# Strides kept as (group, d) on the partitions, 64-row compression products, and the sample convolution moved behind attention

## The reference

```python
s = k_raw[:, :n_str * CMP_STRIDE].reshape(B, n_str, CMP_STRIDE, G, Dh)   # stride, token in stride, group, d
w1r = w1.reshape(CMP_RATIO, CMP_STRIDE, Dh, Dh)                          # 2 halves x 16 x 64 x 64
pre = jnp.einsum('bnlgd,lde->bnge', s[:, 0:nb], w1r[0]) + b1
for r in range(1, CMP_RATIO):
    pre = pre + jnp.einsum('bnlgd,lde->bnge', s[:, r:r + nb], w1r[r])
return jnp.einsum('bnge,ef->bngf', jax.nn.silu(pre), w2)
```

## Time and profile before

| | us |
|---|---|
| median of 3 runs | 831.82 (830.76 to 832.16) |
| the profiled execution, its own time | 829.77 |
| span of its instructions | 828.0 |
| PE busy | 774.4 (94% of the span) |
| DVE busy | 375.8 (45%) |
| ACT busy | 220.5 (27%) |
| POOL busy | 166.9 (20%) |

### The profile page before, as it was taken

One profiled execution on the slowest core, in us unless ns is written; L12 is line 12 of the kernel. 1 busy time (PEld: TensorE's weight loads), 2 busy tenths in 40 slices (PEclk: granted clock), 3 DMA queues, 4 the chain that ended last, 5 costly groups with the idle time before them and its releaser, 6 DMA issues.

```text
span 828.0 us, 11541 instructions
## 1 busy us (share of the span) xinstructions
PE 774.4 (94%) x4479; PEld 541.6 (65%) x4479; DVE 375.8 (45%) x799; ACT 220.5 (27%) x480; POOL 166.9 (20%) x270
## 2 busy tenths in 40 slices
PE   5999999997999999999999999999999899998763
PEld 3657778876766667777767777774456855555431
DVE  2201899999778880111006552231227632222106
ACT  3000324252256662233125640000001112221113
POOL 2338447100200006000005420002000213222010
PEclk9999999998999999999999999999999999999889
DMA  9676445130270005152214529703105999999847
GB/s 314 166 15 189 140 102 159 45 112 1 68 277 2 2 2 180 51 179 76 77 51 132 177 89 297 288 1 115 51 26 208 385 386 413 406 405 395 322 149 263
DMA packets 87505, 138.98 MB, mean 168 GB/s; under 512 B 25493, under 2 KB 60465, under 8 KB 86287
## 3 DMA queue, kind: packets, MB, share of 16 engines
q1 hardware_dynamic: 71439, 101.41, 35.7%
q0 software_dynamic: 11392, 32.71, 13.3%
q10 hardware_dynamic: 4616, 4.08, 1.6%
HBM read 132.00 MB, written 21.14 MB: 185 GB/s over the span
## 4 chain that ended last, share of the span: by engine, by line
PE 79%; DMA 8%; DVE 7%; issue 4%; SPq 1%; ACT 1%; ACTq 0%; POOL 0%; DVEq 0%; POOLq 0%
PE ps L1914 17%; PE ps L2099 15%; PE ps L2357 7%; PE ps L2435 6%; PE ps L1938 5%; PE ps L2012 4%; PE ps L2451 3%; DMA mgT<-w_up 2%; PE ps L2142 2%; PE ps L2117 2%; DVE cv L1399 2%; PE ps L2130 2%; DMA arena<-w_up 2%; DMA arena<-yscratch 2%; PE ps L2425 1%
## 5 line engine op out<-in xcount | busy, mean ns | idle before, releaser
L2099 PE MATMUL ps<-xT,keep 128*128 128x288 f32 x512 | 126.9, 408 | 0.8 <-ACT h L1210 0.5
L2099 PEld LDWEIGHTS ps<-xT,keep 128*128 128x128 f32 x512 | 96.7, 190 | 27.2 <-ACT h L1210 0.9
L1914 PE MATMUL ps<-xT,arena 128*128 128x288 f32 x384 | 95.4, 408 | 0.6 <-DVE keep L1492 0.6
L1914 PEld LDWEIGHTS ps<-xT,arena 128*128 128x128 f32 x384 | 72.3, 190 | 20.0 <-issue 0.8
L1399 DVE SCALAR_TENSOR_TENSOR cv<-keep,cv 128x512 f32<-128x512 f32 x120 | 83.7, 749 | 1.4
L2357 PE MATMUL ps<-arena,xT 128*128 128x512 f32 x128 | 55.4, 592 | 0.0
L2435 PE MATMUL ps<-keep,mgT 128*64 128x256 f32 x224 | 42.9, 396 | 2.1 <-DMA mgT<-w_up 2.1
L1938 PE MATMUL ps<-mgT,xT 128*128 128x512 f32 (+1 forms) x128 | 44.4, 507 | 0.0
L2357 PEld LDWEIGHTS ps<-arena,xT 128*128 128x128 f32 x128 | 24.2, 190 | 29.2 <-issue 29.1
L842 ACT ACTIVATE mgT<-ps 64x512 f32<-64x512 f32 x56 | 33.1, 591 | 32.3 <-PE ps L1992 31.7
L1280 ACT ACTIVATE keep<-h 128x1024 f32<-128x1024 f32 (+1 forms) x5 | 5.3, 1057 | 130.1 <-DVE h L1705 121.5
(11 more groups left out here) (409 smaller groups left out, 1337.7 us busy)
## 6 DMA issues: line engine op xcount, KB each, us to landing
arena<-w_down SPq DMA_DIRECT2D x19, 512.0 KB, 16.7
keep<-w_in SPq DMA_DIRECT2D x16, 512.0 KB, 3.9
arena<-w_gate SPq DMA_DIRECT2D x15, 512.0 KB, 8.6
arena<-w_up SPq DMA_DIRECT2D x15, 512.0 KB, 12.2
keep<-w_gate SPq DMA_DIRECT2D x14, 512.0 KB, 11.5
keep<-w_up SPq DMA_DIRECT2D x14, 512.0 KB, 17.0
h<-x_prompt SPq DMA_DIRECT2D x8, 512.0 KB, 5.2
arena<-w_in SPq DMA_DIRECT2D x8, 512.0 KB, 8.0
```

What stands on the lines that cost most here:

```text
L1914: last = mm(tokens(j)[:, b, :], weights(k), halves(x[:, k, :])[:, b, :], start=k == 0, stop=k == n_k - 1)
L2099: last = mm(out[:, 0:half], wmg[n // 2 % 3][:, k, :], xT[:, k, (n % 2) * half:(n % 2 + 1) * half], start=k == 0, stop=k == KD - 1, skip_gr ...
```

## The change

1. XT becomes partition (group, d), then token in stride, stride: what a turned job has already. `spread` and `spread_own` become one copy each.
2. The compression product takes one token of the stride at a time: 16 matmuls of 64 rows for each group and column range in place of 8 of 128 rows, the two groups alternating, group 0 in the rows 0 to 63 of the array and group 1 in 64 to 127. Both groups' jobs are claimed together and filled by the last pair.
3. The weights stand twice, once for each group's partitions, in three pieces of 8, 4 and 4 tokens in free memory: 12 transfers instead of 2 for each of w_ck1 and w_cv1, of 1 MB instead of 0.5 MB.
4. Before attention PE does the last query projection and the last two rope products ahead of the second compression product. The small products on the compressed values go behind the first two units' scores, in place of the 18 unread transposes, and their evictions stand between the exps (ACT) and after the first normalization (DVE). A table AT_ENTRY gives the slots there, and attention waits slot by slot instead of for all four.
5. The samples' convolution stands in one piece behind attention. "mean" goes from behind 4 gates to behind 8, "var" from behind 10 to behind 14, and the third kind of cached keys from behind 8 to behind 6.
6. The first two merge weights and the gathers of cached keys no longer wait for the samples' convolution; the third merge weight gets a new place and waits for the last rope job.

```diff
-        XT = cut(0, NKV, KD, STR, base=mg_flat)
+        XT = cut(0, 2 * KD, STR, base=mg_flat)
-        w1 = cut(4096, KD, P)
+        w1 = [(8, cut(4096, 8, P)), (4, cut(HPG * (T + SEQ), 4, P, base=h_flat)), (4, cut(2 * KD * STR, 4, P, base=mg_flat))]
+        w1_row = [w[:, x, :] for n, w in w1 for x in range(n)]
...
             def compress_weights(name):
-                for r in range(2):
-                    sp.dma_start(w1[:, :, r * HD:(r + 1) * HD],
-                                 a[name][0, r * 16:(r + 1) * 16].rearrange("(j q) d e -> (q d) j e", q=2)).then_inc(s_w1, 16)
+                x = 0
+                for n, w in w1:
+                    for g in range(NKV):
+                        for r in range(2):
+                            sp.dma_start(w[g * HD:(g + 1) * HD, :, r * HD:(r + 1) * HD],
+                                         a[name][0, r * 16 + x:r * 16 + x + n].rearrange("j d e -> d j e")).then_inc(s_w1, 16)
+                    x += n
...
         def spread(copy, how, j, u):
-            for q in range(2):
-                for g in range(NKV):
-                    v = slot(j)[g * HD:(g + 1) * HD, :].rearrange("p (k q s) -> p k q s", q=2, s=P)[:, :, q, :]
-                    k0 = (u % 2) * (KD // 2)
-                    last = copy(XT[q * HD:(q + 1) * HD, g, k0:k0 + KD // 2, (u // 2) * P:(u // 2 + 1) * P], v, *how)
-            return last
+            rows = slice((u % 2) * KD, (u % 2 + 1) * KD)
+            return copy(XT[:, rows, (u // 2) * P:(u // 2 + 1) * P], slot(j).rearrange("p (k s) -> p k s", s=P), *how)
...
             def compress_first(n):
...
-                for g in range(NKV):
-                    j = first_job(n, g)
+                out = [first_job(n, g) for g in range(NKV)]
+                for j in out:
                     claim(pe, j)
-                    for lo, hi in ((0, STR_S // 2), (STR_S // 2, STR)):
-                        for k in range(KD):
-                            last = mm(strides_at(j)[:, lo:hi], w1[:, k, :], XT[:, g, k, lo:hi], start=k == 0, stop=k == KD - 1)
-                    fill(last, j)
+                for lo, hi in ((0, STR_S // 2), (STR_S // 2, STR)):
+                    for x in range(16):
+                        for g in range(NKV):
+                            r = slice(g * HD, (g + 1) * HD)
+                            last = mm(strides_at(out[g])[:, lo:hi], w1_row[x][r, :], XT[r, x, lo:hi], start=x == 0, stop=x == 15)
+                            if x == 15 and hi == STR:
+                                fill(last, out[g])
...
-            for j in range(J_ATT - SLOTS, J_ATT):
-                result_of(pe, j)
+            result_of(pe, JOB["rope", 2])
             cmp_scores(0)
+            result_of(pe, JOB["w1", 1])
             scores(0)
+            result_of(pe, JOB["w1own", 1])
             scores(1)
-            for _ in range(18):
-                tr(turned[0][:, 0:P], ident[:, :], ident[:, :])
+            sample_values()
+            prompt_values()
             cmp_turns(0)
+            result_of(pe, JOB["w2", 1])
...
             keys_turned(0)
+            dve.wait_ge(s_pv, NU)
+            conv_sample(0, DS)
             j = JOB["mean"]
             result_of(dve, j)
...
-            conv_done(pool)
             pool.wait_ge(s_cso, 16 * (1 + DB))
+            result_of(pool, JOB["ga", CC - 2], JOB["ga", CC - 1])
             for b in range(2):
                 gather("cache_k_sel", kraw[b], b, s_kin[b])
```

More of the change, by code:

```diff
@@ L315, in build @@
         qtmp = cut(12416, 2, T)
-        wmg = [cut(1024 * s, KD, P, base=k2) for s in range(3)]
+        wmg = [cut(1024 * s, KD, P, base=k2) for s in range(2)] + [cut(2080, KD, P, base=k3)]
         PT = [cut(6400 + 1024 * s, NKV, 512) for s in range(2)]
@@ L648, in values_window @@
                     sp.dma_start(vwin[:, b, :, :], svw[:, n, :, :]).then_inc(s_vw, 16)
-            conv_done(sp)
+            for c in range(CC):
+                sp.wait_ge(s_tap[c], TAPS)
             take(sp, JOB["cso"])
-            for n in range(3):
+            for n in range(2):
                 mg_weights(n)
+            result_of(sp, JOB["rope", HPG - 1])
+            mg_weights(2)
+            sp.wait_ge(s_anew, CC)
             sp.wait_ge(s_kvout, 16 * N_KVOUT)
@@ L1124, in _ @@
             spread_raw(1, 5, 7)
+            queries(3)
             upper_halves(1)
             compress_silu(1)
-            queries(3)
-            j = JOB["w2", 1]
-            take(act, j)
-            give(nc.scalar.activation(vcS[:, :, :].rearrange("p b n -> p (b n)"), slot(j)[0:HD, :], ACT.Copy), j)
             def merge_gate(n, src):
@@ L1176, in _ @@
             exps(0)
+            j = JOB["w2", 1]
+            take(act, j)
+            give(nc.scalar.activation(vcS[:, :, :].rearrange("p b n -> p (b n)"), slot(j)[0:HD, :], ACT.Copy), j)
             exps(1)
@@ L1212, in _ @@
             keys_turned(0, 0)
-            merge_gates(*range(4))
+            merge_gates(*range(6))
+            keys_turned(0, 2)
+            merge_gates(6, 7)
             j = JOB["mean"]
@@ L1234, in _ @@
                 nc.scalar.activation(cv[:, c, :], cv[:, c, :], ACT.Silu, scale=cng[:, c:c + 1], bias=cnb[:, c:c + 1]).then_inc(s_silc, 1)
-            merge_gates(*range(13, 22))
+            merge_gates(*range(17, 22))
             small_exps(0)
@@ L1501, in _ @@
             rotated(2)
-            conv_sample(0, 5)
+            rotated(3)
             compress_pre(1)
-            conv_sample(5, DS)
-            j = JOB["w2own"]
-            take(dve, j)
-            for g in range(NKV):
-                r = slice(g * STR_P, (g + 1) * STR_P)
-                last = V.tensor_copy(vcB[r, g * HD:(g + 1) * HD], slot(j)[r, g * HD:(g + 1) * HD])
-            give(last, j)
-            rotated(3)
             def maxima(u):
@@ L1556, in _ @@
             normalize(0)
+            j = JOB["w2own"]
+            take(dve, j)
+            for g in range(NKV):
+                r = slice(g * STR_P, (g + 1) * STR_P)
+                last = V.tensor_copy(vcB[r, g * HD:(g + 1) * HD], own_values(j)[r, g * HD:(g + 1) * HD])
+            give(last, j)
             for u in range(NU):
```

76 lines of the change are left out of this document (39 added, 37 removed).

## The result

| kernel | median us (lowest to highest, runs) | ratio to before, 95% interval |
|---|---|---|
| before | 831.82 (829.53 to 834.29, 7) | 1 |
| changed | 824.84 (823.56 to 828.2, 7) | 0.9916, 0.9897 to 0.9936 |

Forecast were 822.7 us, in a range of 819.2 to 827.0. The kernel is 7.0 us faster (5.3 to 8.6), where 9.1 were forecast. The profiled execution took 824.84 us, its span is 823.1.

What follows compares the result with a forecast made beforehand. The chain of waits was taken to run through PE, then DVE up to the second compression product. First score 9.2 us earlier less 0.1 for the entry gives 9.1; 831.82 less 9.1 is 822.7 us, range 819.2 to 827.0.

Steps and rivals of the forecast that it cites:

- Product: Each compression product takes 14.9 us at full clock because half-height pairs overlap; bounds 14.7 to 18.2, without overlap 29.4.
- PE late next: Ahead of the second compression product PE becomes late; third queries wait 1.65 us, the product runs from 200.2 to 215.1.
- Entry: From the second product's end to the second unit's turns: 12.0 us where it was 11.9; bounds 10.5 to 14.
- larger gain: Rival: attention's entry takes 10.5 us as value products keep the clock full; 1.5 to 2 us more, 820.9; chance 0.10.
- Behind attention: The samples' convolution, 20.3 us on DVE, ends at 337.8 before PE wants it for "mean" at 348.1; costs nothing.
- The sum ahead of attention: Attention's first score 9.2 us earlier, less 0.1 for the entry: 9.1 us gained.
- a gain ahead of attention should reach the end undiminished: Later stages start from results of earlier ones, so the whole 9.1 us was counted in the total.
- cheaper evictions: On DVE up to the second product, single copies replace the strides' evictions and save 4.1 us against 1.05 lost.
- ahead of attention the same 20.3 us on DVE gave PE nothing: Moving the samples' convolution from ahead of attention gains PE nothing; its wait at 224.29 was for the last rotation only.
- No overlap: Rival in the compression products: the array's halves don't work together; 29.4 us more, 852.1; chance 0.06.
- POOL and DVE hold each other up: Rival behind attention: DVE slowed, PE waits 10 us for "mean", 832.7; chance 0.03. If POOL suffers, nothing is lost.
- The clock or the entry takes a part back: Rival in attention's entry: PE's three waits halve the clock for longer, price 2 to 4 us, 825.5; chance 0.15.

Runs made afterwards that it cites:

- serial_groups: Changed kernel with its 128 half-height products issued group after group, so neighbours never use different row halves; 851.91 us, ratio 1.0215.
- order_only: Changed kernel with its new order but the strides' old layout, copies and full-height products; 822.0 us, ratio 0.9874.
- after_c: Changed kernel run a third time without an edit; 825.66 us, ratio 0.9904 to the kernel before.
- shift: Changed kernel with 64 unread transposes added on PE ahead of the second compression product; 832.3 us, ratio 0.9997.
- the repeats: The changed kernel run two more times without an edit; 825.29 and 825.66 us, ratios 0.9919 and 0.9904 to the kernel before.
- layout_only: Kernel before with only the strides' new layout, half-height product pairs and twelve weight transfers, in the old order; 828.4 us, ratio 0.9946.
- conv_front: Changed kernel with the samples' convolution back at its old place ahead of attention, five steps before the second bias addition, three behind; 832.43 us, ratio 1.0008.
- conv_gaps: Changed kernel with the samples' convolution ahead of attention, placed into DVE's two idle stretches as three and five steps; 824.53 us, ratio 0.9914.

## Why the prediction was right, and where it was off

- **Product.** 14.9 forecast, 14.88 measured, twice, and serial_groups shows that it rests on the overlap. The rule of the Trainium skill (TensorE: Matmul & The Clock Gate, LDWEIGHTS), an estimate of 13.7 us for the 128 loads, was just below the streaming time; the trace agrees as far as 128 loads fit into 14.88 us, 116 ns each, while one is recorded with 187.
- **PE late next.** The product was to start at 200.2 and end at 215.1; it did at 199.14 and 214.02, and the front of this execution was 1.22 us early by itself, so they are 0.1 to 0.2 late. The third queries start 1.03 us later than in order_only (175.47 against 174.44, with the same start of the first), the 1.05 of the forecast; that their wait is 1.14 and not 1.65 comes from PE itself, which arrives half a microsecond later.
- **Entry.** 12.0 forecast, 12.03 measured. The clock was not as forecast: 0.81 was expected in this stage, 1.00 was granted. The number held all the same: full speed didn't give the 1.5 us of the rival "larger gain" because PE isn't what is waited for there. Its waits of 0.44 and 1.03 us end with ACT and DVE.
- **Behind attention.** "mean" without a wait, at 337.81 for a forecast of about 339 (337.8 with the early front).
- **The sum ahead of attention.** 9.1 forecast, 9.02 measured between the landmarks (8.8 against the two later profiles of before; 8.1 to 8.3 in after_c).
- **Off: the total.** 9.1 forecast, 7.0 measured, and 6.7 and 8.0 by the ratios of the repeats. The step that failed, in its size only, is "a gain ahead of attention should reach the end undiminished". It holds up to the merged output projection (246.14 us behind the first merge gate in every profile), and of a shift of 7 us (shift) no loss can be seen in the total. But 1 to 2 us are missing behind that projection, among the routing and the experts. Why stays open. Known is that this stage differed by 6.6 us between three executions of the kernel before (265.9 to 272.5), more than what is missing, and that the last expert's products, above, are where most of the difference on average shows. A smaller part may lie ahead of attention, where after_c gained 0.74 less. With an interval of 5.3 to 8.6 us for the gain, 9.1 is just outside.
- **Off: what the steps are worth.** I counted 4.1 us for cheaper evictions. Only the old order has a use for them (3.4 us up to the second product in layout_only); in the new one they are worth nothing, and order_only shows that the layout costs 1.42 us. And "ahead of attention the same 20.3 us on DVE gave PE nothing" holds in the old order alone. In the new one, conv_front loses 8.27 us by it. The forecast came out because I walked through the new order as a whole, not because the parts were worth what I said of them.
- **The rivals.** No overlap and the larger gain didn't come. Of "POOL and DVE hold each other up" the harmless half came: POOL was held up, and "mean" did not wait. "The clock or the entry takes a part back" has about the right price, but at the wrong place: the clock was full throughout the entry in two of the three profiles, and in the third, after_c, its fall cost 0.74 us.

## What to carry to other kernels

Two changes aimed at the same wait don't add up: before counting a cheaper copy as a gain, look for what covers it once the order is new, and measure each half alone. An engine that is idle in two known stretches (here 7.4 and 12.7 us) can take work in pieces that fit, and three of the eight pieces, left behind the second stretch, cost 8 us. Compare landmarks inside the traces where the total scatters more than the effect, and look at more than one profile of each kernel: the last stages of one and the same kernel differed by 6.6 us.

## What the runs showed of the hardware

Pairs of half-height float32 products ran for 64 matmuls (128 instructions in the rows) at almost the rate of one full-height matmul per pair: 3.72 us for 32 instructions of 64 x 256 in both halves, 3.72 for 16 of them in one half. The whole surcharge of a product was 0.20 us (14.88 against 14.68).

A wait on PE costs twice. With 3.83 us of idle time ahead of it the second product took 17.17, 16.59 and 16.54 us in three profiles of before, and 14.83 in order_only, with the same matmuls and no idle time ahead. In conv_front the granted clock was 0.51 over the 10.3 us from 222.0, so the lower of its two levels (1.2 GHz) for practically all of it; PE was idle up to 229.07, and the work behind the wait still ran at that level.

When POOL works beside DVE's convolution, it is mostly POOL that is held up. Its line L990 by the groups of 304 to 345 us, in the changed kernel, took 588 ns on average and a copy 778, where the same operations took 443 and 286 before:

```profile
L990 POOL TENSOR_SCALAR keep<-keep,pmod 128x64 f32<-128x64 f32 x7 | 4.0, 588 | 0.0
...
L993 POOL COPY keep<-keep 128x128 f32<-128x128 f32 x2 | 1.6, 778 | 0.0
```

With the convolution ahead of attention, in conv_gaps, the two are back at 448 and 289 ns. DVE's products beside POOL's work stayed at 1.18 to 1.32 us. The Trainium skill (GPSIMD Engine Reference, Specifications) has the two engines contend when a DVE instruction has two SBUF inputs, as these products have, and does not say there which waits; here it was POOL, up to the 0.13 us by which one product of DVE was longer.
